# A hybrid decoder step on one core: router weights and a state copy issued earlier, loads reordered, extra-block tables and output-projection weights moved

## The reference, cut to what matters

```python
mixed = jnp.concatenate([o_nsa, o_rwkv.astype(o_nsa.dtype)], axis=-1) @ lp['w_out']
x = x + gt1 * mixed
h2 = (rmsnorm(x, lp['norm2']) * (1.0 + sc2) + sh2).reshape(B * T, D)
eid, ew = hier_route(h2, lp['w_router_group'], lp['b_router_group'], lp['w_router_expert'], lp['b_router_expert'])
ffn = moe_ffn(h2, eid, ew, lp['w_gate'], lp['w_up'], lp['w_down']).reshape(B, T, D)
x = x + gt2 * ffn
```

## Time and profile before

| | |
|---|---|
| Runs | 2964.82, 2967.74, 2974.37 us |
| Profiled execution, its own time | 2967.66 us |
| its span, first to last instruction | 2965.6 us |
| PE busy / PEld busy | 2501.3 us (84%) / 1874.7 us (63%) |
| DVE / ACT / POOL busy | 771.0 / 301.2 / 60.9 us |
| granted clock of TensorE, mean | 0.898 of full speed |
| DMA | 680.37 MB, mean 229 GB/s |

### The profile page before, as it was taken

One profiled execution on the slowest core, in us unless ns is written; L12 is line 12 of the kernel. 1 busy time (PEld: TensorE's weight loads), 2 busy tenths in 40 slices (PEclk: granted clock), 3 DMA queues, 4 the chain that ended last, 5 costly groups with the idle time before them and its releaser, 6 DMA issues. The chain is left out here.

```text
span 2965.6 us, 51304 instructions
## 1 busy us (share of the span) xinstructions
PE 2501.3 (84%) x22349; PEld 1874.7 (63%) x22349; DVE 771.0 (26%) x1929; ACT 301.2 (10%) x681; POOL 60.9 (2%) x100
## 2 busy tenths in 40 slices
PE   5999997799997457766667794699999999999996
PEld 4776775577775356745545573577677677677674
DVE  0112110300003754444545112311112211112215
ACT  0101011000000300011322001001000101100101
POOL 0000000000000100001012000000000000000000
PEclk9999998799997766675778896799999999999998
DMA  5888885143331200013766414299999999999990
GB/s 216 343 310 312 308 312 190 61 158 125 113 113 43 29 3 5 5 33 83 231 250 235 170 57 174 95 423 407 389 396 402 395 396 398 394 398 402 393 375 33
DMA packets 179396, 680.37 MB, mean 229 GB/s; under 512 B 36667, under 2 KB 37644, under 8 KB 140524
## 3 DMA queue, kind: packets, MB, share of 16 engines
q1 hardware_dynamic: 171778, 640.42, 55.6%
q0 software_dynamic: 4608, 33.56, 3.4%
q10 hardware_dynamic: 2884, 4.50, 0.4%
HBM read 669.27 MB, written 17.50 MB: 232 GB/s over the span
## 5 line engine op out<-in xcount | busy, mean ns | idle before, releaser
L571 PE MATMUL bank<-sb_hT,sb_w_in 128*128 128x296 f32 x1408 | 353.5, 414 | 3.9 <-PEq L462 3.9
L571 PEld LDWEIGHTS bank<-sb_hT,sb_w_in 128*128 128x128 f32 x1408 | 269.0, 191 | 88.5 <-issue 5.8
L2451 PE MATMUL bank<-sb_gate_w,sb_x_picked 128*64 128x256 f32 x2048 | 322.2, 379 | 0.7 <-DMA sb_up_w<-in_w_up_dram 0.7
L2451 PE MATMUL bank<-sb_up_w,sb_x_picked 128*64 128x256 f32 x2048 | 322.1, 379 | 0.0
L2476 PE MATMUL bank<-sb_down_w,sb_hiddenT 128*64 128x512 f32 x1024 | 226.8, 594 | 9.0 <-ACT sb_x_picked L2511 9.0
L397 PE MATMUL bank<-sb_cmp_xT,sb_cmp_w 128*128 128x254 f32 x1024 | 223.4, 379 | 6.7 <-ACT sb_cmp_xT L213 5.8
L397 PEld LDWEIGHTS bank<-sb_cmp_xT,sb_cmp_w 128*128 128x128 f32 x1024 | 193.2, 190 | 39.0 <-ACT sb_cmp_xT L213 8.4
L2451 PEld LDWEIGHTS bank<-sb_gate_w,sb_x_picked 128*64 128x64 f32 x2048 | 175.2, 137 | 59.9 <-issue 17.1
L2435 PE MATMUL bank<-sb_select,sb_h2rows 128*128 128x128 f32 x1632 | 189.6, 279 | 18.6 <-DVE sb_give L2545 18.6
L2451 PEld LDWEIGHTS bank<-sb_up_w,sb_x_picked 128*64 128x64 f32 x2048 | 175.4, 137 | 45.6
L2435 PEld LDWEIGHTS bank<-sb_select,sb_h2rows 128*128 128x128 f32 x1632 | 186.4, 194 | 24.8 <-DVE sb_give L2545 18.7
(11 more groups left out here) (533 smaller groups left out, 2413.5 us busy)
## 6 DMA issues: line engine op xcount, KB each, us to landing
sb_gate_w<-in_w_gate_dram SPq DMA_DIRECT2D x64, 2048.0 KB, 11.7
sb_up_w<-in_w_up_dram SPq DMA_DIRECT2D x64, 2048.0 KB, 16.2
sb_down_w<-in_w_down_dram SPq DMA_DIRECT2D x64, 2048.0 KB, 9.8
sb_w_ada<-in_w_ada_dram SPq DMA_DIRECT2D x48, 2048.0 KB, 10.8
sb_w_in<-in_w_in_dram SPq DMA_DIRECT2D x11, 4096.0 KB, 13.2
sb_cmp_raw<-in_cache_cmp_kv_dram SPq DMA_DIRECT2D x128, 256.0 KB, 7.6
sb_w_out<-in_w_out_dram SPq DMA_DIRECT2D x4, 4096.0 KB, 12.8
sb_sample_kv<-in_state_win_kv_dram SPq DMA_DIRECT2D x8, 1024.0 KB, 10.8
```

What stands on the lines that cost most here:

```text
L571: ins = pe.matmul(k.bank[m][:, 0:NX], w[r][:, t, m * P:(m + 1) * P], k.hT[:, t, :], start=(t == 0), stop=(t == KT - 1))
L2451: ins = pe.matmul(bank[b][64 * half:64 * half + 64, col:col + 256], x[:, t, b * 64:b * 64 + 64], w[i][:, t % CK, half * 256:half * 256 + 256],
```

## The change

It does these things:

1. In `phase_scan`, SP first issues the 8128 KB copy and the router weights in four DMAs; half of them go to a part of `mod` that is no longer used, half to a new tile. 21 semaphores of this stage are given back and reused later, and POOL clears them at the start of `phase_rows`.
2. In `write_rows`, the copy is gone and `prefetch()` stands ahead of the row stores.
3. Chunks 0 to 2 of `w_out` are loaded in the last turns of the samples' attention, into page buffers that those turns free; chunk 3 in `phase_out`.
4. In `phase_route`, POOL clears the bias tile first, and SP issues the two bias DMAs ahead of expert 0. Ranks and weights are made in their final tables, so two copies go; one copy of counts is new.
5. The extra-block tables move into `phase_moe`, on DVE behind `select(0)`. SP's main loop takes the expert's number from its loop counter. All engines wait for the tables after the main loop.

```diff
 # phase_scan, SP
+                sp.dma_start(A["win_kv_sample"][0, :, 0:WINL - TS].rearrange("b s kv g d -> b (s kv g d)"),
+                             A["state_win_kv"][0, :, TS:WINL].rearrange("b s kv g d -> b (s kv g d)")).then_inc(k.s_kept, 16)
+                    for i, w in enumerate(k.wrt):
+                        for at, n, src in ((0, NGRP, A["w_router_group"]), (NGRP, NEXP, A["w_router_expert"])):
+                            sp.dma_start(w[:, :, at:at + n], src[0].rearrange("(k p) n -> p k n", p=P)[:, i * KT // 2:(i + 1) * KT // 2, :]).then_inc(k.s_wrt, 16)
                 sp.wait_ge(s_oa, 2)
 # phase_rows, POOL
+                for spent in k.scan_spent:
+                    pool.sem_clear(spent)
 # write_rows
-    out(A["win_kv_sample"][0, :, 0:WINL - TS].rearrange("b s kv g d -> b (s kv g d)"),
-        A["state_win_kv"][0, :, TS:WINL].rearrange("b s kv g d -> b (s kv g d)"))
+    prefetch()
     sp.wait_ge(k.s_rows_zero, 1)
...
-    prefetch()
     sp.wait_ge(s_o, 16 * n_out[0])
 # phase_attend_samples, SP, at the end
+                for n in range(3):
+                    sp.wait_ge(s_av, N_TURN - 2 + n)
+                    load_w_out(k, A, sp, n)
+def load_w_out(k, A, sp, n):
+    view = A["w_out"][0].rearrange("(k p) n -> p k n", p=P)
+    for j in range(4):
+        sp.dma_start(k.raw[(4 * n + 4 + j) % N_UNITS][:, :, :], view[:, 4 * j:4 * j + 4, n * 512:(n + 1) * 512])\
+            .then_inc(k.s_w_out[n], 16)
 # phase_out, SP and PE
-                for n in range(N_CH):
-                    if n >= 2:
-                        sp.wait_ge(s_tile, 4 * (n - 1))
-                    sp.dma_start(w[n % 2][:, :, :], w_view[:, :, n * CH:(n + 1) * CH]).then_inc(s_w[n % 2], 16)
+                sp.wait_ge(s_tile, 4)
+                load_w_out(k, A, sp, 3)
-                        pe.wait_ge(s_w[n % 2], 16 * (n // 2 + 1))
+                        pe.wait_ge(k.s_w_out[n], 64)
 # phase_route, SP
-                load_expert(k, A, sp, 0)
-                with nc.allow_non_contiguous_dma(reason="small router weights"):
-                    sp.dma_start(w[:, :, 0:NGRP], A["w_router_group"][0].rearrange("(k p) n -> p k n", p=P)).then_inc(s_w, 16)
-                    sp.dma_start(w[:, :, NGRP:NL], A["w_router_expert"][0].rearrange("(k p) n -> p k n", p=P)).then_inc(s_w, 16)
                 sp.wait_ge(s_i, 1)
                 sp.dma_start(bias[0:1, 0:NGRP], A["b_router_group"]).then_inc(s_w, 16)
                 sp.dma_start(bias[0:1, NGRP:NL], A["b_router_expert"]).then_inc(s_w, 16)
+                load_expert(k, A, sp, 0)
 # phase_route, PE
-                pe.wait_ge(s_w, 64)
+                pe.wait_ge(k.s_wrt, 64)
+                pe.wait_ge(s_w, 32)
 # phase_route, DVE: L2290 to L2324 leave; extra_blocks(k, dve, c) holds L2292 to L2324
-                step(dve.tensor_copy(k.slot[:, :, 0:NEXP], rank[:, :, :]))
-                step(dve.tensor_copy(k.weight[:, :, 0:NEXP], wt[:, :, :]))
...
+                step(dve.tensor_copy(k.count[:, :], k.bank[0][:, 64:64 + NEXP]))
 # phase_moe
+            eng.wait_ge(s_extra, 1)
             with eng.If(eng.value_load(k.expert[0:1, N_BLK:N_BLK + 1], min_val=0, max_val=N_OVER) > 0):
...
+                load(0, 1, 1)
+                with sp.Fori(1, NEXP // 2) as n:
+                    for b in range(2):
+                        load(n, b, 2 * n + b)
...
                 select(0)
+                extra_blocks(k, dve, c).then_inc(s_extra, 1)
                 both(dve, turn, lambda pairs: add(pairs - 1))
 # phase_final, SP, at the end
+                sp.wait_ge(k.s_kept, 16)
```

More of the change, by code:

```diff
@@ L2128 @@
 NGRP, NEXP, EPG = 4, 32, 8
+NL = NGRP + NEXP
 SLOTS = 64
@@ L2315, in _ @@
-                tt(ex[:, 3, :], ex[:, 3, :], ex[:, 2, :], ALU.add)
-                ts(ef[:, over], ex[:, 0, :], float(NEXP - 1), None, ALU.min)
-                tt(pick[:, :, :], by_o(ef[:, 0:NEXP]), by_e(ef[:, over]), ALU.is_equal)
-                for i in range(NTT):
-                    for table, dst in ((rank, k.slot), (wt, k.weight)):
-                        tt(ind[:, :, :], pick[:, :, :], by_o(table[:, i, :]), ALU.mult)
-                        red(dst[:, i, over], ind[:, :, :], ALU.add)
@@ L2322, in _, with extra_blocks @@
-                tt(k.slot[:, :, over], k.slot[:, :, over], ex[:, 3, :].unsqueeze(1).to_broadcast([P, NTT, N_OVER]),
-                   ALU.subtract)
-                step(dve.tensor_copy(k.expert[:, :], ef[0:1, :]))
+                step(dve.tensor_copy(k.count[:, :], k.bank[0][:, 64:64 + NEXP]))
+def extra_blocks(k, dve, c):
+    sb = lambda name, shape: k.sb(name, shape, F32, c)
+    nb, cum, excl = sb("extra_blocks", [P, NEXP]), sb("extra_cum", [P, NEXP]), sb("extra_tmp", [P, NEXP])
+    ind, pick = sb("extra_ind", [P, N_OVER, NEXP]), sb("extra_pick", [P, N_OVER, NEXP])
+    ex, onum, ef = sb("extra_scalars", [P, 4, N_OVER]), k.onum, k.ef
+    step = k.steps.chain(dve)
+    tt = lambda out, a, b, op: step(dve.tensor_tensor(out, a, b, op))
+    ts = lambda out, a, s1, s2, o1, o2=None: step(dve.tensor_scalar(out, a, s1, s2, o1, o2) if o2 else
+                                                  dve.tensor_scalar(out, a, s1, s2, o1))
+    red = lambda out, a, op: step(dve.tensor_reduce(out, a, AX.X, op))
+    cnt = k.count[:, :]
+    ts(nb[:, :], cnt, SLOTS + 0.5, None, ALU.is_gt)
+    for j in range(2, (NT - 1) // SLOTS + 1):
+        step(dve.scalar_tensor_tensor(out=nb[:, :], in0=cnt, scalar=j * SLOTS + 0.5, in1=nb[:, :], op0=ALU.is_gt,
+                                      op1=ALU.add))
+    step(dve.tensor_copy(cum[:, :], nb[:, :]))
+    for s in (1, 2, 4, 8, 16):
+        step(dve.tensor_copy(excl[:, :], cum[:, :]))
+        tt(cum[:, s:NEXP], excl[:, s:NEXP], excl[:, 0:NEXP - s], ALU.add)
+    step(dve.tensor_copy(ef[:, N_BLK:N_BLK + 1], cum[:, NEXP - 1:NEXP]))
+    over = slice(NEXP, N_BLK)
+    by_o = lambda v: v.unsqueeze(1).to_broadcast([P, N_OVER, NEXP])
+    by_e = lambda v: v.unsqueeze(2).to_broadcast([P, N_OVER, NEXP])
+    tt(ind[:, :, :], by_o(cum[:, :]), by_e(onum[:, :]), ALU.is_le)
+    red(ex[:, 0, :], ind[:, :, :], ALU.add)
+    tt(pick[:, :, :], ind[:, :, :], by_o(nb[:, :]), ALU.mult)
+    red(ex[:, 1, :], pick[:, :, :], ALU.add)
+    ts(ex[:, 2, :], ex[:, 0, :], NEXP - 0.5, 1.0e3, ALU.is_gt, ALU.mult)
+    tt(ex[:, 3, :], onum[:, :], ex[:, 1, :], ALU.subtract)
+    ts(ex[:, 3, :], ex[:, 3, :], float(SLOTS), float(SLOTS), ALU.mult, ALU.add)
+    tt(ex[:, 3, :], ex[:, 3, :], ex[:, 2, :], ALU.add)
+    ts(ef[:, over], ex[:, 0, :], float(NEXP - 1), None, ALU.min)
+    tt(pick[:, :, :], by_o(ef[:, 0:NEXP]), by_e(ef[:, over]), ALU.is_equal)
+    for i in range(NTT):
+        for dst in (k.slot, k.weight):
+            tt(ind[:, :, :], pick[:, :, :], by_o(dst[:, i, 0:NEXP]), ALU.mult)
+            red(dst[:, i, over], ind[:, :, :], ALU.add)
+    tt(k.slot[:, :, over], k.slot[:, :, over], ex[:, 3, :].unsqueeze(1).to_broadcast([P, NTT, N_OVER]),
+       ALU.subtract)
+    return dve.tensor_copy(k.expert[:, :], ef[0:1, :])
@@ L2400, in _, with load @@
             def _(sp):
-                def turn(n, fresh, before):
+                def load(n, b, e):
+                    load_expert(k, A, sp, e, lambda i: sp.wait_ge((s_half, s_gu, s_yh, s_y)[i], 2 * n + b))
+                load(0, 1, 1)
+                with sp.Fori(1, NEXP // 2) as n:
                     for b in range(2):
-                        if fresh and b == 0:
-                            continue
-                        e = sp.value_load(k.expert[0:1, bass.ds(2 * n + b, 1)], min_val=0, max_val=NEXP - 1)
-                        load_expert(k, A, sp, e, lambda i: sp.wait_ge((s_half, s_gu, s_yh, s_y)[i], 2 * n + b))
-                both(sp, turn)
+                        load(n, b, 2 * n + b)
+                sp.wait_ge(s_extra, 1)
+                with sp.If(sp.value_load(k.expert[0:1, N_BLK:N_BLK + 1], min_val=0, max_val=N_OVER) > 0):
+                    with sp.Fori(NEXP // 2, N_BLK // 2) as n:
+                        for b in range(2):
+                            load(n, b, sp.value_load(k.expert[0:1, bass.ds(2 * n + b, 1)], min_val=0, max_val=NEXP - 1))
             @block.tensor
```

77 lines of the change are left out of this document (31 added, 46 removed).

## The result

After the change the median is 2898.47 us (2896.77 to 2907.68, 4 runs), against 2971.05 for the kernel before in the same session (4 runs): ratio 0.9762, 95% interval 0.9737 to 0.9787. The profiled execution took 2897.25 us with a span of 2895.5. Profile against profile that is 70.4 us less, where 79.7 were forecast. The time lies in the range; the profiled execution is 9.3 us above the point, the median 10.5 us.

A forecast was written before the change was run, and what follows sets the result against it. PE bounds the experts' stage, which only shifts; gains come from waits on the only path. 25.2 + 12.6 + 27.4 + 3.5 + 13.0 - 2 = 79.7 us off 2967.7 gives 2888 us, range 2878 to 2905.

The forecast's parts named there:

- Part 1: Border into samples' attention: samples' loads ahead of row stores, copy gone; gain 25.2 us, bounds 7 and 30.
- the window wait: Samples' attention: PE's 7.05 us wait for the windows at L1779 goes, about 1 us of it given back.
- the upper bound's mechanism: Samples' attention: PE, not slowed by idling, does 8.7 us of products at up to twice the speed; bound 30 us.
- Part 2: Border into the output projection: w_out loaded early into page buffers; gain 12.6 us, bounds 0 and 12.6.
- So PE starts at 1644.6: Output projection: w_out's first chunk lands at about 1636, before PE wants it, for a gain of 12.6 us.
- Parts 3 and 4: Routing: early router weights and bias first, 27.4 us, plus clock 3.5; extra-block tables off the path, 13.0.
- The clock's 3.5 us: Router: products start at the upper clock, which falls 3.5 us in; gain 3.5 us, bounds 0 and 8.5.
- L397's row: Products of nearly the router's shape kept PE busy at clock 0.50; cited against the router keeping the upper clock.
- The row of 3.2 us: Routing: the bias took 3.2 us from 1840.54 to 1843.71, so issued first it would be there by 1812.5.
- Part 5: Recurrence: copy and router weights moved there are covered by idle DMA engines; cost 2 us, bounds 0 and 22.
- The rival of the disturbed code stream: Recurrence: copy and short runs occupy engines bringing PE its code; up to 20 us beyond the 2; chance 0.12.
- its bound of a fifth of the copy's interval: Recurrence: cost bounded by a fifth of each transfer interval, 0.7 us for 33 packets, 22 us in all.

The follow-up runs named there:

- The warmed router: Kernel after the change plus 48 unread PE products in the norm ahead of the routing: ratio 0.9787 to the kernel before; routing 28.98 us, not 31.93.

## Why the prediction came out as it did

**Part 1, right at the border, too small behind it, and partly wrong in reason.** The border gave the 19.1 us forecast and the window wait went. It was the copy alone; I had ascribed it to the copy and the order together. In all the part gave 31.8 us, where I had 25.2 and an upper bound of 30. The samples' attention gained 12.7 us and not 6.05. Its clock was 0.89 on the mean and had been 0.81; in twelve other profiles without that border wait it took 143.4 to 150.2 us at 0.89 to 0.83. PE is busy 96.7 us in this stage and not 105.9 for the same work. That is the upper bound's mechanism, which I had left out of the value and, in the bound, had given to the first 8.7 us of products only. How much of it is the edit's and how much the clock's scatter stays open.

**Part 2, mis-sized by a fifth.** 12.6 us forecast, 10.15 found, and 8.0 to 8.9 in seven of the nine kernels with three chunks early. The step that failed is "So PE starts at 1644.6". I had written that a stage starts when all streams of the last one have ended, and then priced w_out's arrival but not the time that SP needs to issue it: SP was still issuing chunk 2, and PE started 0.45 us after it had done. One chunk early instead of three avoids that.

**Parts 3 and 4, right in size, part 3 wrong in its reason.** 43.9 us forecast, 44.2 found. The clock's 3.5 us were 3.1, and the fall came within the router as L397's row had suggested. Uncovered tables cost 12.6 us, forecast 13. What I had not seen is how much hung on the order: with expert 0 first the bias takes 28.8 us. The row of 3.2 us held because expert 0 had already landed. And "L2168, all short runs, had held the queue for 28.32 us" gives the wrong cause: the runs land within 2.9 us when nothing is ahead of them, and what held them was expert 0's 12.6 MB. The number came out because the change moved both the weights and the bias out from behind expert 0. That was luck in the reasoning: a change that loaded only the weights early would have missed by 28 us.
The Trainium skill, TensorE: Matmul & The Clock Gate, section What's actually happening, gives the lower clock to an idle array and the upper one to a busy array. The warmed router speaks against it for this shape: PE was busy without a pause and fell to the lower level all the same.

**Part 5, the step that failed.** "Take 2, near the lower end, because the engines are asked for so little of what they can move": 8.6 us on the mean of ten profiles, 12.1 in the one compared. The demand in GB/s was the wrong measure. What counts is how late one code packet is: a small rate is no cover where PE stands still as soon as a packet is late, as it does for 2.9 to 3.7 us at L951. The rival of the disturbed code stream, given 0.12, is what happened, and its bound of a fifth of the copy's interval held on the mean: 8.6 us in the 45.6 in which it runs. In the pair compared it did not, with 12.1. The intervals themselves were too long: 81 us for the copy was 45.6, and 28.3 us for the short runs was under 3 without the copy. The short runs are 4160 packets and cost under 1 us, the copy is 136, so it is not the number of packets that costs. That the sum landed within the range is partly luck: part 1 gave 6.65 us too much and part 5 took 10.1 too much.
The Trainium skill, DMA: Bandwidth & Descriptors, section Queues, rings and completion order, says that an engine takes turns between queues by whole packets. With that, a 16.4 KB code packet would wait for a copy packet of 2.5 us. The trace agrees as far as it goes: 8 code packets came in 50 us instead of 10 or 11, and PE stood still until late ones had landed. No row shows a packet waiting its turn.

**Not foreseen.** Prompt attention, 3.05 us more: clock 0.74 instead of 0.75, and in other profiles of the same instructions 72.2 to 87.3 us, longer where the granted clock is lower; why it falls where it falls stays open. `phase_rows`, 2.7 us more: 46.5 and 47.1 us in the two kernels without the router's tile and the cleared semaphores, 49.2 to 50.2 in the twelve with them. SP's issue of the second weight's long DMA is the visible part:

```profile
1354.71 4.80 SPq L1311 DMA_DIRECT2D sb_cp_w<-in_cmp_v_w_dram  x1
```

```profile
1367.74 6.61 SPq L1318 DMA_DIRECT2D sb_cp_w<-in_cmp_v_w_dram  x1
```

Neither the clears' place nor the loads in the recurrence cause it: the stage took 49.7 us with both loads gone from the recurrence. Whether the tiles' places or the semaphores do was not tried and stays open.

## What to carry to other kernels

An idle DMA engine is not free for a bulk copy if PE runs long unrolled code beside it: count the packets of the instruction queue and put large transfers where PE has few instructions to fetch. Behind the projection's last load it fetches 1 or 2 packets in 50 us, where the recurrence has 10 or 11. A small load that ends a wait goes out ahead of the large ones. A long issue is a sign of what stands ahead in the queue, not of the load that is being issued. Where a stage waits for all streams, count the time that SP needs to issue early loads as well as their landing, and leave it nothing to issue at the border. Take each part back alone: here two lines of order held 28 us once the weights were early, and another reordering held nothing.

## What the runs showed of the hardware

- A copy of 8128 KB in packets of 61 KB on the mean cost PE 8.6 us in a stretch where code flowed at 3 to 5 GB/s; 4160 packets of short runs in the same place, without the copy, cost under 1 us.
- With several MB queued, SP needed up to 4.6 us to issue one DMA of 1 MB; the first four of the same kernel had taken 0.4 to 0.8 us each. In nine profiles the next stage's first product came 0.44 to 0.45 us after the last such issue, 1.5 to 5.0 us behind the last computation; 0.3 us behind it where SP had issued all before.
- A router load of 128 KB in short runs landed within 2.9 us with nothing ahead of it. Behind 12.6 MB the issue of 256 KB of them alone took 28.3 us, and the router's bias, 144 bytes, behind the same 12.6 MB took 28.8 us to land.
- The same prompt attention took 72.2 us at a granted clock of 0.81 and 87.3 at 0.64. Differences between builds of that size need a look at the clock before any other cause.
- Router products of 36 columns kept PE busy and still fell to the lower clock, 3 to 6 us in; 23 us of wide products ahead of them moved the fall from within or at the end of the first third of the 96 products to the middle of the second.
